# Gates as row sums of the transposed ada weights, all low parts on VectorE, and fourteen slots for the first loads

## What is computed

```python
c_act = jax.nn.silu(c)                                   # (1, 2048)
for i in range(2):
    mod = (c_act @ ada_w[i] + ada_b[i])[:, None, :]      # (1, 1, 6144)
    shift, scale, gate = jnp.split(mod, 3, axis=-1)
    h = rmsnorm(x, norm_g[i]) * (1.0 + scale) + shift
    y = retention_branch(h, ...) if i == 0 else mla_branch(h, ...)
    x = x + gate * y
x = rmsnorm(x, final_norm_g)
```

## Time and profile before

| | |
|---|---|
| time, median of 3 runs (lowest, highest) | 2304.78 us (2304.28, 2305.55) |
| the profiled execution's own time, its span | 2307.71 us, 2305.8 us |
| TensorE, VectorE, ScalarE, GpSimd busy | 97%, 66%, 45%, 11% |
| DMA, HBM read | 65.1% of 16 engines, 498 MB |
| mean granted TensorE clock | 0.988 |

### The profile page before, as it was taken

How to read it: one execution, slowest core, us unless ns; L and a number is a source line. 1 busy time by engine, 2 the same in 40 slices (tenths; PEclk the granted TensorE clock), 3 DMA queues, 4 the chain that set the end, 5 groups by cost and what they waited for, 6 DMA issues and landing times.

```text
span 2305.8 us, 27060 instructions
## 1 busy us (share of the span) xinstructions
PE 2237.0 (97%) x10364; PEld 1848.1 (80%) x10364; DVE 1510.6 (66%) x1844; ACT 1034.6 (45%) x1344; POOL 261.7 (11%) x148
## 2 busy tenths in 40 slices
PE   6999999999999989999989999999999999999999
PEld 4877777878887778889868788877888888888887
DVE  7999777668876869655655555565454555555554
ACT  3543354443444445545444355444444344444442
POOL 1222123222222100000020200000000000000000
PEclk9999999999999989999999999999999999999999
DMA  8998587778887659735445554554666656666664
GB/s 297 350 328 318 178 298 235 260 276 307 292 300 256 234 188 347 251 115 170 147 145 208 164 175 139 173 184 153 186 184 190 194 189 191 188 186 192 191 185 145
DMA packets 140087, 501.92 MB, mean 218 GB/s; under 512 B 15667, under 2 KB 16179, under 8 KB 139443
## 3 DMA queue, kind: packets, MB, share of 16 engines
q1 hardware_dynamic: 139958, 500.20, 65.1%
HBM read 498.04 MB, written 2.10 MB: 217 GB/s over the span
## 4 chain that ended last, share of the span: by engine, by line
PE 82%; DVE 9%; DMA 3%; issue 2%; ACT 2%; POOL 1%; SPq 0%; DVEq 0%; ACTq 0%; POOLq 0%
PE ps L983 66%; PE ps L994 6%; DVE wlo L1527 2%; PE ps L1053 2%; DVE raw L1555 2%; PE ps L1008 2%; DMA raw<-in_ret_in 2%; PE ps L1045 1%; ACT whi L1219 1%; DVE arena L1676 1%; DVE x L1747 1%; DVE arena L1739 1%; DVE arena L1685 1%; PE ps L1144 0%; POOL arena L1950 0%
## 5 line engine op out<-in xcount | busy, mean ns | idle before, releaser
L1527 DVE TENSOR_TENSOR wlo<-raw,whi 128x1024 fp32r<-128x1024 f32 (+1 forms) x689 | 845.4, 1233 | 583.5 <-ACT whi L1219 580.5
L1219 ACT ACTIVATE whi<-raw 128x1024 fp32r<-128x1024 f32 (+1 forms) x753 | 783.9, 1045 | 892.7 <-PE ps L983 651.0
L983 PE MATMUL ps<-whi,ahi 128*128 128x512 f32 x2590 | 828.3, 400 | 15.9 <-DVE alo L1590 6.8
L983 PE MATMUL ps<-wlo,ahi 128*128 128x512 f32 x2590 | 808.3, 392 | 13.7 <-DVE wlo L1527 12.3
L983 PE MATMUL ps<-whi,alo 128*128 128x512 f32 x2590 | 807.7, 392 | 0.0
L983 PEld LDWEIGHTS ps<-wlo,ahi 128*128 128x128 f32 x2590 | 488.4, 189 | 121.3 <-DVE wlo L1527 15.6
L983 PEld LDWEIGHTS ps<-whi,alo 128*128 128x128 f32 x2590 | 490.0, 189 | 104.5 <-issue 0.2
L983 PEld LDWEIGHTS ps<-whi,ahi 128*128 128x128 f32 x2590 | 479.7, 190 | 116.9 <-DVE alo L1590 7.5
L1946 POOL TENSOR_TENSOR wlo<-raw,whi 128x1024 fp32r<-128x1024 f32 x64 | 164.0, 2563 | 555.7 <-ACT whi L1219 555.7
L1555 DVE SCALAR_TENSOR_TENSOR raw<-raw,arena 128x1024 f32<-128x1024 f32 x128 | 175.1, 1376 | 17.6 <-ACT arena L1240 13.3
L994 PE MATMUL ps<-whi,ahi 128*128 128x512 f32 x306 | 121.2, 396 | 3.7 <-DVE alo L1590 3.7
(11 more groups left out here) (188 smaller groups left out, 1134.3 us busy)
## 6 DMA issues: line engine op xcount, KB each, us to landing
raw<-in_mlp SPq DMA_DIRECT2D x256, 512.0 KB, 3.6
raw<-in_ret_in SPq DMA_DIRECT2D x192, 512.0 KB, 4.8
raw<-in_ada_t SPq DMA_DIRECT2D x128, 512.0 KB, 5.1
raw<-in_in SPq DMA_DIRECT2D x80, 512.0 KB, 4.2
raw<-in_ada SPq DMA_DIRECT2D x64, 512.0 KB, 5.0
raw<-in_ret_out SPq DMA_DIRECT2D x64, 512.0 KB, 5.1
raw<-in_mla_in SPq DMA_DIRECT2D x48, 512.0 KB, 4.7
raw<-in_mla_out SPq DMA_DIRECT2D x32, 512.0 KB, 4.3
```

What stands on the lines that cost most here:

```text
L983: mm = e.matmul(acc_[:, :], (ahi, alo, ahi)[m][:, slot, kb, tb * P:(tb + 1) * P], (whi, whi, wlo)[m][:, q, chunk(n)], start=first and m == ...
L1219: e.activation(whi[:, q, 0:ncol], raw_of(n)[:, 0:ncol], ACT.Copy).then_inc(*s_hi.up(i))
L1527: e.tensor_tensor(wlo[:, q, 0:ncol], raw_of(n)[:, 0:ncol], whi[:, q, 0:ncol].bitcast(F32), ALU.subtract).then_inc(*s_lo.up(i))
```

## The change

- `POOLED` and GpSimd's split go; VectorE does all low parts.
- The gate tiles are loaded from the transposed weights as well and summed by `adt` (a third pair of sums per kb). `gate_sum` adds halves and bias for four kb, `gate_row` turns four such columns to a row of 512 on all partitions by four fp32 matmuls with the identity, and ScalarE copies it to `gate`. `ada`, `ada_done`, the accumulators, `cact` and `gate_bias` go.
- `c_wide` stays whole for layer 1's shift and scale. Only layer 1's gates need a new c row (`c_late`, on other space), loaded and activated before `ret_out` 2.
- The first 24 loads use 14 slots: six of `raw` and eight on space for the decay tables, g, v and v next. The first partial sums wait until that is free.
- x is loaded first on SyncE's queue. c row, columns and identity are issued by ScalarE. Positions, frequencies and mask come after the side-by-side part of phase 0, the angle tables are made from phase 1 on.
- The decay tables of part 0 go into x (`first_decays`), the others are one load after part 1's g (`decays`), and `x_again` comes after part 2's qk.
- `mod_first` and `mods` handle pairs of kb from kb 4 on, and ScalarE makes the modulated input (Identity to scratch, then Copy to `ahi`); VectorE only subtracts.
- The `drain` of side jobs after the first projection goes.

The core of the diff:

```diff
-POOLED = 256
+EARLY = 14
...
-    ada = [("ada", 0, g, k) for g in (4, 5) for k in range(16)]
+    ada = [("adt", 0, kb, 2, h) for kb in range(16) for h in range(2)]
     ada += [("adt", 1, kb, c, h) for kb in range(16) for c in range(2) for h in range(2)]
-    gate = [("ada", 1, g, k) for g in (4, 5) for k in range(16)]
+    gate = [("adt", 1, kb, 2, h) for kb in range(16) for h in range(2)]
...
+            _, layer, kb, c, h = plan[n]
+            do("adt", layer, kb, c, h, n)
+            if c == 1 and h and layer == 0 and kb < 4:
+                do("mods", layer, kb, 1)
+                ready.append(range(kb, kb + 1))
+            elif c == 1 and h and kb % 2:
+                do("mods", layer, kb - 1, 2)
+                if layer == 0:
+                    ready.append(range(kb - 1, kb + 1))
+            elif c == 2 and h and kb % 4 == 3:
+                do("gate_sum", layer, kb // 4)
+                urgent.append((at["used"] + 3, lambda layer=layer, j=kb // 4: gate_row(layer, j)))
...
-    side += [lambda: do("angles"), lambda: do("reduced"), lambda: do("tables")]
...
+        if ph == 0:
+            do("later_in")
+        if ph == 1:
+            side += [lambda: do("angles"), lambda: do("reduced"), lambda: do("tables")]
...
-    drain()
-    do("x_again")
+    do("first_decays")
...
-    do("decays", 0)
     for p in range(4):
         if p >= 2:
             gemm(("qk", p), 0, "h0", range(16), 1024, evac_to("act", "qk_out", p))
+            if p == 2:
+                do("x_again")
...
         if p:
-            do("decays", p)
             gemm(("g", p), 0, "h0", range(16), 1024, evac_to("act", "g_out", p))
         if p == 1:
-            do("gate_bias", 0)
+            do("decays")
...
+        def lane_of(n):
+            return n % EARLY if n < 24 else (n - 24 + 24 % EARLY) % RAW
...
+            def first_decays():
+                w.wait_ge(*s_at.on(("h0", 15)))
+                e.dma_start(x[:, 0, 0:512], K[:, K_D:K_D + 512]).then_inc(*s_in["decay0"].up("in"))
...
             def x_again():
-                w.wait_ge(*s_at.on(("h0", 15)))
+                w.wait_ge(*s_vec.on(("sT", 0, 1)))
...
             def c_again():
-                w.wait_ge(*s_col.on((0, 5, 1)))
-                e.dma_start(c_wide, ins["c_row"].to_broadcast([P, D])).then_inc(*s_in["c_again"].up("in"))
+                w.wait_ge(*s_att.on(("ret_values", 3, 1, 1)))
+                e.dma_start(c_late, ins["c_row"].to_broadcast([P, D])).then_inc(*s_in["c_wide"].up("in"))
...
+            def gate_row(layer, j, bank):
+                acc_ = empty(bank)
+                w.wait_ge(*s_vec.on(("gate_sum", layer, j)))
+                for i in range(4):
+                    mm = e.matmul(acc_[:, i * P:(i + 1) * P], gate_col[:, layer, 4 * j + i:4 * j + i + 1].to_broadcast([P, P]), ident[:, :],
+                                  start=True, stop=True)
...
+            def mod_first(kbs):
+                k0, n = kbs[0], len(kbs)
+                t = scr[:, kbs[0] % 4 * 256:kbs[0] % 4 * 256 + 256 * n]
+                w.wait_ge(*s_act.on(("xn", k0 // 2)))
+                w.wait_ge(*s_vec.on(("mod", 0, kbs[-1])))
...
+                for j, kb in enumerate(kbs):
+                    a = e.activation(t[:, j * 256:j * 256 + 256], xn(kb), ACT.Identity, scale=mod[:, 0, 1, kb:kb + 1], bias=mod[:, 0, 0, kb:kb + 1])
...
+                e.activation(flat(ahi[:, 0, k0:k0 + n, :]), t, ACT.Copy).then_inc(*s_ahi.up(*[("h0", kb) for kb in kbs]))
...
-            def split(i, n):
-                if low_of(i) is s_lo:
-                    return
-                q, ncol = i % RING, plan[n][3]
-                w.wait_ge(*s_hi.on(i))
-                e.tensor_tensor(wlo[:, q, 0:ncol], raw_of(n)[:, 0:ncol], whi[:, q, 0:ncol].bitcast(F32), ALU.subtract).then_inc(*s_lop.up(i))
```

More of the change, by code:

```diff
@@ L184, in pump, with gate_row @@
                 continue
[L185 to L206, removed]
+            _, layer, kb, c, h = plan[n]
[10 more added lines that the diff above has]
+                urgent.append((at["used"] + 3, lambda layer=layer, j=kb // 4: gate_row(layer, j)))
+    def gate_row(layer, j):
+        bank = take()
+        do("gate_row", layer, j, bank)
+        give(bank, "act", ("gate", layer, j))
     def mod_to(kb):
         while kb not in modulated:
-            modulated.add(ready[0])
+            modulated.update(ready[0])
             do("mod_first", ready.popleft())
@@ L455, in schedule @@
     drain()
+    do("c_again")
     for g in range(2):
@@ L705, in fused_blocks @@
         ps = [ctx.enter_context(nc.psum_tensor(f"ps{i}", [P, 512], F32)) for i in range(8)]
-        s_raw = [signal(f"raw_landed{i}", 16) for i in range(RAW)]
-        small = ("cols", "ident", "pos", "freq", "c_row", "c_again", "x00", "x01", "x10", "x11", "x_again", "mask", "decay0", "decay1", "decay2", "decay3", "gate0", "gate1",
+        s_raw = [signal(f"raw_landed{i}", 16) for i in range(EARLY)]
+        small = ("cols", "ident", "pos", "freq", "c_row", "c_wide", "x00", "x01", "x10", "x11", "x_again", "mask", "decay0", "decay",
                  "final_g", "ws", "bmask")
@@ L797, in fused_blocks @@
         htmp1 = flat(S1)[:, 0:1024]
-        late_accs = [flat(v1)[:, i * 1024:i * 1024 + 1024] for i in range(2)]
+        c_late = flat(v1)
         fg = flat(qT1)
@@ L959, in x_add @@
                     e.dma_start(out[0, tb * P:(tb + 1) * P, chunk(c)], x[:, tb, chunk(c)]).then_inc(*s_out.up((tb, c)))
-            walk(dict(opening=opening, load=load, x_in=x_in, x_again=x_again, c_again=c_again, mask_in=mask_in, decays=decays, gate_bias=gate_bias, final_g=final_g,
+            walk(dict(opening=opening, load=load, later_in=later_in, x_again=x_again, c_again=c_again, first_decays=first_decays, decays=decays, final_g=final_g,
                       small_loads=small_loads, x_add=x_add))
@@ L1021, in krope @@
                 mm.then_inc(*s_mm.up(("used", i), "krope"))
-            def ada_done(layer, g, got):
-                a = acc(layer, g)
-                w.wait_ge(*s_ada.on(("bias", layer, g)))
-                for j, bank in enumerate(got):
-                    e.matmul(empty(bank)[:, :], ones[:, :], a[:, chunk(j)], start=True, stop=True).then_inc(*s_col.up((layer, g, j)))
+            def gate_row(layer, j, bank):
[4 more added lines that the diff above has]
+                                  start=True, stop=True)
+                mm.then_inc(*s_col.up((layer, j)))
             def opening(got):
@@ L1032, in opening @@
                 for j, bank in enumerate(got):
-                    e.matmul(empty(bank)[:, :], ones[0:1, :], gate[0:1, chunk(j)], start=True, stop=True).then_inc(*s_col.up(("c", j)))
+                    e.matmul(empty(bank)[:, :], ones[0:1, :], c_wide[0:1, chunk(j)], start=True, stop=True).then_inc(*s_col.up(("c", j)))
             def norm_turn(src, k2, bank):
@@ L2138, in layout @@
     g["x"] = a["x"]
-    g["ada_b"] = ab
     g["final_norm_g"] = a["final_norm_g"]
```

241 lines of the change are left out of this document (102 added, 139 removed).

## The result

The changed kernel takes **2284.98 us** (median of 4, 2284.34 to 2285.52); the kernel before, on the same chip, 2304.53 us (median of 4, 2303.54 to 2305.55). The ratio is 0.9915, with a 95% interval from 0.9898 to 0.9932: 19.6 us less. The forecast was 2282, the range 2268 to 2297.

What follows compares the result with a forecast made beforehand. TensorE, busy 97% of the span, bounds the kernel, so only its idle and slow stretches pay: -4 (0 to 60 us), -7 (60 to 220), -4 (260 to 300), -8 (460 to 480), -23 in all; forecast 2282 us, range 2268 to 2297.

Steps and rivals of the forecast that it cites:

- the median of the runs lies 1.0 us below that span: Last step of the sum: took the predicted span of 2282.8 us to a median of 2281.8, forecast 2282.
- Part 1: Low parts from GpSimd to VectorE: 17.1 us of splits offset by 17.7 us of stretch from 55 to 212 us; 0.
- 0 elsewhere: Outside 55 to 212 us, moving GpSimd's splits to VectorE costs about 0, since VectorE has room after 200 us.
- more than forecast: Rival: front -15, holes -6 and -8.5, evacuations near 780 us without GpSimd's hold -3; 2272 us, chance 0.15.
- Part 2: First input modulated on ScalarE, 60 to 220 us: VectorE falls to 147 us, DMA bounds at 153; -7 us.
- VectorE gets +4 here: 60 to 220 us: angle tables, eleven instructions, some 4 us, move to the second phase and add 4 us to VectorE.
- the 153 us: 60 to 220 us: DMA's time for 53.4 MB at 0.349 MB/us, taken as the new bound there.
- Part 3: Fourteen slots, x first, c_row from ScalarE's queue, tables later: 0 to 60 us gains -4 us, slots alone little.
- Part 4: Auxiliary loads, 260 to 300 us: SyncE's 19.4 us wait at decays(0) goes; -4 us, with x_again hidden.
- next late: Once SyncE's 19.4 us wait goes, VectorE, busy with ropes, is next late; TensorE asked for the result 2 us after.
- no SyncE wait over 10 us before 300 us: Sign that the forecast is right: SyncE has no wait longer than 10 us in the first 300 us.
- Part 5: Gates as row sums: the 13.3 us wait for layer 1's reloaded c row vanishes, 460 to 480 us; -8 us.

Runs made afterwards that it cites:

- experiment 1: The kernel before with every low part made by VectorE, GpSimd's splits gone, nothing else changed; 2298.66 us, ratio 0.9978.
- Experiments 4 and 5: The changed kernel with the angle tables made ahead of the first phase (4: 2283.65 us) or ahead of the fourth phase (5: 2282.24 us).
- experiment 4: The changed kernel with the angle tables and their loads back ahead of the first phase, before kb 3; 2283.65 us, ratio 0.9911.
- experiment 10: The changed kernel with angle tables ahead of the fourth phase and GpSimd making every fourth low part of weights 64 to 95; 2279.53 us, ratio 0.9895.

## Why the prediction was right, and where it wasn't

**Span and median.** The sum gave a span of 2282.8 us; it is 2282.6. That the two agree to 0.2 us is in part luck, since the two profiled executions lie apart by 3.6 us more than the medians. The median is 3 us above the forecast because of the step "the median of the runs lies 1.0 us below that span". Between an execution's time and its span lie 1.9 us before (2307.71 and 2305.8) and 1.7 after (2284.34 and 2282.6): the median of after had to be the span plus 1.7 and the scatter. The profiled execution of the kernel before was simply 3 us slower than its median, and I carried this accident over as if it were a property. By medians the change is worth 19.6 us, by the traces 23.2, and the forecast was 23.

**Part 1: the cause right, "0 elsewhere" wrong.** L1529, the form of L1555, takes 1.216 us on average from 60 to 220 us, 1.488 before; the 14 splits of that stretch cost VectorE nothing, as said (experiment 1: busy for 152.1 us from 60 to 220, 153.8 before). The Trainium skill, GPSIMD Engine Reference, section 1 (Specifications), which puts contention where a VectorE instruction has two SBUF inputs, is borne out: L1676, with one input in PSUM, took 0.679 us beside GpSimd's splits and 0.684 without (experiment 1). L1587, with a single SBUF input, was held too, 0.672 us and 0.409 without; the same section names instructions in a 2-port performance mode as its other case, and whether L1587 runs in one no row shows. What failed is the step from VectorE's sum to the path. VectorE's busy time is a sum over quiet and full moments; the splits of GpSimd hold it where row sums, evacuations and splits meet. There the removal was worth 6.3 us in the kernel before (weights 38 to 50), 2.1 up to weight 50 in the changed one, and 5.1 to 9.5 (weights 244 to 258). Where GpSimd's splits had run beside partial sums from PSUM, which they do not stretch, it cost 2.2, and 1.8 more at weight 236. By medians the part is worth 5.8 us alone and 4.6 on top of the rest; the places add up to 10.6 and to 3.1 us, so single places are known to a few us only. The rival "more than forecast" had this place, with -3; it should have been in the sum.

**Part 2: -7 was -1.2.** The step that failed is "VectorE gets +4 here", a sum over 160 us, where the order of one burst decided. VectorE's load fell as worked out (34.8 + 45.6 + 46.7 + 18.8 = 145.9 us, 147 predicted). DMA was not the bound either: 0.84 from 100 to 150 us, and from 60 to 100 us it moved 385 GB/s, where the 153 us were worked out with 349. ScalarE's list is in order, and as before it contains a wait for `mods` at each kb, or now pair, with the copies to `whi` behind. Eight of the twelve instructions of the tables (2.9 us) stood ahead of one `mods` and made this wait 5.1 us; the other four made ScalarE wait 2.1 us more, and TensorE saw it. Experiments 4 and 5 show -5.8 and -5.9 between weights 8 and 50 without them, and with the tables late the predicted -7 is there. It is not shown to be part 2's: part 1 alone gave 6.3 of it, with the tables where they had been. Either relief of VectorE brings TensorE near its own pace in that stretch (115.2 to 116.3 us between weights 8 and 50 in the six kernels without GpSimd's splits there and without tables in the second phase), and the sum had put the whole of it under one of them and 0 under the other. No run takes the modulated input off ScalarE alone. I had costed the longer chain of ScalarE only for kb 0 and 1, "0.5 us".

**Part 3: -4 was -4.6, for the reasons given.** Chain of the changed kernel, 0 to 60 us (against rows 3):

```profile
3.29 7.18 PE ps L1020 x8
...
24.81 0.34 DVE alo L1568
...
25.20 4.93 PE ps L968 x12
...
52.27 0.42 DVE alo L1568
```

kb 3's `alo` is at 52.27 us, near 52 as predicted, 55.64 before. The start is 25.20 in both, because the c row landed 0.5 us later in this execution. The tables are most of it: back in front they cost 3.3 us by weight 8 (experiment 4). Slots alone bring nothing here, as said; but I then put their whole value at that and overlooked weights 33 to 38, where they are worth 2.9 us. The rule cited, that DMAs of all issuers interleave on the same engines (DMA: Bandwidth & Descriptors, "Issuing engines are not separate DMA queues" in the Trainium skill), is not contradicted: a c row beside x lands no sooner from one queue than from the other.

**Part 4: -4 was -3.3 (weights 75 to 84); putting the wait back costs 3.9 there.** What was named as next late, VectorE with ropes, showed itself at weights 72 to 75 as part 1's cost. The sign "no SyncE wait over 10 us before 300 us" did not come true to the letter: one of 17.0 us, at 30 us, is that of a queue that has filled its fourteen slots and waits for the first row sums. ScalarE waited for weights for 2.3 us in all from 20 to 60 us, so it cost nothing. SyncE's waits from 0 to 300 us:

```profile
...
SPq L913 <- DVE raw L1529: 64.1, 41, 17.0
```

`x_again` is hidden: landed in 10.0 us, with ScalarE's longest wait for a weight 1.5 us from 300 to 420 us.

**Part 5: -8 was -8.3 (weights 137 to 140).** TensorE's side was taken as 0. In layer 0 the old sums took 3.8 us and the new rows 4.2, first the kernel before, then after, TensorE by line and form from 200 to 820 us:

```profile
L1027 PE MATMUL ps<-arena,ones 128*128 128x512 f32 x8 | 3.8, 592 | 0.0
```
```profile
L1012 PE MATMUL ps<-ident,gate_col 128*128 128x128 f32 x32 | 4.2, 274 | 0.0
```

So the forecast of the total owes much to luck, to errors that cancelled in the traces: +5.8 in the front, +2.2 at the ropes and +2.0 after weight 140 (1.8 of it at weight 236) against -10.2 before layer 1.

## What to carry to other kernels

A helper engine should be costed by what it does to the busy one's instructions, and then placed: here it pays where its work runs beside instructions of the busy engine that it doesn't stretch, those that read PSUM. When work is moved within lists that engines walk in order, ask which wait it lengthens and what stands behind that wait; a sum over the stage says nothing about it. And tie a forecast to the median by the time that lies around the span, not by how the one profiled execution happened to fall.

## What the runs showed of the hardware

- 64 GpSimd splits of 2.56 us on average cost VectorE 74 us, 1.16 us for each, and a split on VectorE itself takes 1.22 (experiment 1). So taken over all 64, handing them over relieved VectorE of nearly nothing.
- What is held depends on where the inputs lie: beside GpSimd's splits a form with both inputs in SBUF went from 0.688 to 0.880 us on average, one of the same size with an input in PSUM stayed at 0.68 (experiment 10).
- A row sum, multiplication and reduction over 1024 columns from two SBUF inputs, takes 1.216 us, the same as a plain subtraction of that size (1.221 us).
- Two waits of TensorE of 1.7 and 1.2 us, which left it busy for 1.5 of the 4 us from 800 to 804, went ahead of 4 us at a granted clock of 0.50 in which it was busy throughout. After a single wait of 1.2 us at 780 us the clock stayed at 1.00, and so it did with one wait of 0.4 us in the same work of experiment 1.
- An 8 KB load landed between 1.6 and 2.5 us after its issue; from which of two queues it came made no difference that stands out of this.
